# Hybrid decoder layer with hierarchical MoE: pair weights stored in four parts, first eight experts requested without a gather

## The reference

```
h  = rmsnorm(x, g_mix);  z = h @ w_in                    # 1024 -> 2048, four mixers of 256 columns
x  = x + concat(conv_a, pool, conv_c, gated_mlp) @ w_out
h  = rmsnorm(x, g_ffn)
g  = argmax of 4 group logits;  two best of the 8 experts of that group
w2 = softmax(two best logits) * softmax(group logits)[g]
x  = x + sum over the two experts of w2 * (silu(h @ w_gate) * (h @ w_up)) @ w_down
y  = rmsnorm(x, g_final)
```

## Time and profile before

| | us |
|---|---|
| median of 3 runs | 636.04 |
| lowest and highest of them | 634.98, 638.97 |
| profiled execution | 636.99 |
| span in its profile | 634.7 |
| busy TensorE products, share of the span | 570.7, 90% |
| busy VectorE, share | 462.3, 73% |
| busy ScalarE, share | 275.7, 43% |
| busy GpSimd, share | 143.8, 23% |
| moved by the transfers | 120.45 MB |

### The profile page before, as it was taken

One profiled execution on the slowest core, in us unless ns is written; L12 is line 12 of the kernel. 1 busy time (PEld: TensorE's weight loads), 2 busy tenths in 40 slices (PEclk: granted clock), 3 DMA queues, 4 the chain that ended last, 5 costly groups with the idle time before them and its releaser, 6 DMA issues.

```text
span 634.7 us, 10552 instructions
## 1 busy us (share of the span) xinstructions
PE 570.7 (90%) x3479; PEld 497.4 (78%) x3479; DVE 462.3 (73%) x726; ACT 275.7 (43%) x432; POOL 143.8 (23%) x178
## 2 busy tenths in 40 slices
PE   8899999999999998999999957999998989898800
PEld 6799999997998896888888746888877868677500
DVE  4938997999999668366665687888876756576525
ACT  6642112320413355322221265767765654565444
POOL 4300002000000000000000233656554545444200
PEclk9999999999999999999999969999999998899955
DMA  8760211120203204867443369999999999995359
GB/s 308 139 144 9 67 34 33 34 78 12 67 9 134 67 1 134 269 237 268 178 156 144 101 186 378 328 299 332 339 326 299 376 304 328 328 317 199 60 206 360
DMA packets 58023, 120.45 MB, mean 190 GB/s; under 512 B 12963, under 2 KB 31272, under 8 KB 57961
## 3 DMA queue, kind: packets, MB, share of 16 engines
q1 hardware_dynamic: 49077, 101.36, 46.9%
q0 software_dynamic: 6720, 17.85, 11.7%
q10 hardware_dynamic: 2164, 0.51, 0.4%
HBM read 95.19 MB, written 29.61 MB: 197 GB/s over the span
## 4 chain that ended last, share of the span: by engine, by line
PE 34%; SPq 19%; DVE 16%; DMA 7%; issue 3%; ACT 2%; POOL 0%; DVEq 0%; POOLq 0%; ACTq 0%
SPq L542 18%; PE ps L2123 13%; PE ps L1945 8%; DMA at_wfirst<-in_expert_w_up 3%; DVE at_mixP L1347 2%; PE ps L2272 2%; PE ps L2187 2%; PE ps L2248 1%; DVE at_x L1848 1%; PE ps L2250 1%; PE ps L2249 1%; DVE at_hT L1306 1%; DVE at_lnsq L1533 1%; DMA scratch_out<-at_outb,at_gcol 1%; PE ps L1873 1%
## 5 line engine op out<-in xcount | busy, mean ns | idle before, releaser
L1945 PE MATMUL ps<-at_hT,at_ring 128*128 128x384 f32 x936 | 164.8, 333 | 0.0
L1945 PEld LDWEIGHTS ps<-at_hT,at_ring 128*128 128x128 f32 x936 | 155.3, 188 | 5.2 <-issue 5.0
L2123 PE MATMUL ps<-at_hT,at_mring 128*128 128x512 f32 (+1 forms) x432 | 102.7, 393 | 2.0 <-DVE at_mring L1501 1.3
L2123 PEld LDWEIGHTS ps<-at_hT,at_mring 128*128 128x128 f32 (+1 forms) x432 | 77.3, 182 | 21.2 <-DVE at_mring L1501 1.7
L2248 PE MATMUL ps<-at_whi,at_hTm 128*128 128x256 f32 x280 | 83.1, 297 | 0.1
L2250 PE MATMUL ps<-at_whi,at_hTm_lo 128*128 128x256 f32 x280 | 80.8, 289 | 0.0
L1347 DVE SCALAR_TENSOR_TENSOR at_mixP<-at_uc,sb_par,at_mixP 128x1024 f32<-128x1024 f32 x60 | 77.4, 1289 | 2.1
L1188 POOL DMA_INDIRECT at_xg<-scratch_h,at_tab x32 | 54.8, 1713 | 72.1 <-DVE at_actv L1709 67.4
L1743 DVE TENSOR_TENSOR at_wlater_lo<-at_wlater,at_whi 128x1024 fp32r<-128x1024 f32 x40 | 48.8, 1221 | 25.3 <-ACT at_whi L958 25.1
L2248 PEld LDWEIGHTS ps<-at_whi,at_hTm 128*128 128x128 f32 x280 | 54.9, 196 | 0.6 <-DVE at_hTm_lo L1734 0.3
L2250 PEld LDWEIGHTS ps<-at_whi,at_hTm_lo 128*128 128x128 f32 x280 | 54.7, 195 | 0.0
(11 more groups left out here) (267 smaller groups left out, 859.6 us busy)
## 6 DMA issues: line engine op xcount, KB each, us to landing
at_wlater<-in_expert_w_gate SPq DMA_DIRECT2D x20, 512.0 KB, 10.6
at_wlater<-in_expert_w_up SPq DMA_DIRECT2D x20, 512.0 KB, 23.9
at_wlater<-in_expert_w_down SPq DMA_DIRECT2D x20, 512.0 KB, 24.2
at_raw<-in_w_in SPq DMA_DIRECT2D x16, 512.0 KB, 3.9
scratch_h<-at_wk SPq DMA_DIRECT2D x8, 1024.0 KB, 5.9
at_wfirst<-in_expert_w_gate SPq DMA_DIRECT2D x15, 512.0 KB, 9.4
at_wfirst<-in_expert_w_up SPq DMA_DIRECT2D x15, 512.0 KB, 21.3
at_wfirst<-in_expert_w_down SPq DMA_DIRECT2D x15, 512.0 KB, 21.3
```

The source lines that it names most:

```text
L1945: mm = pe.matmul(ps[:, bank + r, 0:t1 - t0], w[:, wpart, k * P:(k + 1) * P], hT[:, hpart, k, t0:t1], start=(m, wpart, hpart) == (0, 0, 0), ...
L2123: mm = pe.matmul(ps[0:n, b + r, :], mring[:, 1 - i % 2, mpart, k * P:k * P + n], wo[:, wpart, k, r * 512:(r + 1) * 512], start=(c, mpart, ...
```

## The change

The gates are stored in four parts instead of three: tiles 0 to 5, tile 6, tile 7, tile 8. ScalarE's queue stores part 0 as before and also the last part, behind its zeroing of the gather buffers; SP stores part 1 ahead of its wait for the last projection and part 2 where both of its parts were. A part of one tile is one store, so there are still five. GpSimd and ScalarE do their work for part 1 one stage earlier. On SP's queue the wait for the first gather is gone, and expert 5 is issued ahead of the store of x1 of tile 8.

```diff
-GATE_PARTS = [(0, 6), (6, LAST), (LAST, TILES)]
+GATE_PARTS = [(0, 6), (6, 7), (7, LAST), (LAST, TILES)]
...
             t0, t1 = GATE_PARTS[part]
             eng.wait_ge(s["gates_ready"], part + 1)
-            for k in range(1 if t0 == LAST else 2):
-                if t0 == LAST:
-                    dst = hs[2 * LAST * P:2 * NT, D:D + 1].rearrange("(p k) o -> p (k o)", k=2)
-                    src = gates[0:NS, LAST, :]
+            for k in range(1 if t1 - t0 == 1 else 2):
+                if t1 - t0 == 1:
+                    n = rows(t0)
+                    dst = hs[2 * t0 * P:2 * (t0 * P + n), D:D + 1].rearrange("(p k) o -> p (k o)", k=2)
+                    src = gates[0:n, t0, :]
...
             for i in range(TILES):
                 if i == LAST:
+                    store_gates(sp, 1)
                     sp.wait_ge(s["o_done"], TILES)
                     expert_block(0, FIRST, expert_at(FIRST), first=True)
...
-            for part in (1, 2):
-                store_gates(sp, part)
+            store_gates(sp, 2)
             expert_block(0, FIRST + 1, expert_at(FIRST + 1), first=True)
+            expert_block(0, FIRST + 2, expert_at(FIRST + 2), first=True)
             store_x1(LAST)
-            sp.wait_ge(gath[0], 16)
-            for j in range(FIRST + 2, LAP):
+            for j in range(FIRST + 3, LAP):
                 expert_block(0, j, expert_at(j), first=True)
...
                 if i == LAST:
                     store_gates(act, 0)
+                    gate_exp(1)
...
-            gate_exp(1)
+            gate_exp(2)
...
                 if n == 2:
-                    gate_exp(2)
+                    gate_exp(3)
...
                    s["xg_zero"])
+            store_gates(act, 3)
...
                 if i == LAST:
                     gate_values(0)
                     gate_terms(1)
+                    gate_values(1)
+                    gate_terms(2)
                 rms(1, i)
-            gate_values(1)
-            gate_terms(2)
             gate_values(2)
+            gate_terms(3)
+            gate_values(3)
```

## The result

The changed kernel takes 641.25 us (median of 11 runs, 637.53 to 643.83). The kernel before, run beside it, has a median of 637.27 us over 11 runs. The ratio is 1.0063, interval 1.0044 to 1.0081: the change costs 4.0 us (0.0063 of 637.27; 2.8 to 5.2). I had forecast 1.1 us less, with a range up to 638.7. The direction was wrong and the time lies outside the range. The outcome is nearest to rival C, to which I had given 0.18: the last tile's gates became the wait. The profiled execution took 642.72 us, with a span of 640.7.

What follows compares the result with a forecast made beforehand. The weight stream on SP's queue, with full DMA engines, was taken as the bound. Filling 2.8 us less 1.5 us new idle gave 1.3 us less, written as 634.9 us against 636.04, range 631.8 to 638.7.

Steps and rivals of the forecast that it cites:

- rival C: Last tile's gates, landing late beside weights, become the first gather's wait; d 6.8 us, loss 2.7 us, 638.7 us; chance 0.18.
- d: How much later the first expert ends, from later gathers and TensorE's clock: 2.8 us, bounds 0 to 5.5.
- Step 1: Tile 6's gates leave SP's late queue; their work and store fall into idle time, price zero.
- Step 2: Last tile's gates go from SP to ScalarE, landing about 378.4 us, 0.8 us before GpSimd's first gather starts.
- Step 3: Expert 4 asked for earlier on SP's queue fills idle DMA time before 388 us: gain 2.8 us, bounds 2.0 to 3.5.
- Rival D: Early weights only stand in their slots, as buffer release is the limit; time stays at 636.0 us; chance 0.12.
- Step 4: First gather meets weights, landing 2.0 us late; 2.3 us for two gathers plus 0.5 us for TensorE's clock dip.
- Rival B: Gather and gates share engines with weights packet by packet; d 0.8 to 1.5 us, about 633.5 us; chance 0.25.
- Step 5: Expert 8's weights wait for the late first expert's buffer, so the queue runs dry: 1.5 us of new idle.

Runs made afterwards that it cites:

- e1_wait_back: The changed kernel with SP's wait for the first gather put back ahead of experts 5 to 7; ratio 1.0050 to the kernel before, +3.2 us.
- e11_one_matrix_ahead: The changed kernel, but SP stores the last gates after only one of expert 4's three matrices, and waits for the first gather before experts 5 to 7; ratio 0.9989 to before.

## Why the prediction was wrong

**The bound was read rightly.** The engines of the transfers are full behind 406 us, expert 8's request ties the stream to the first gather, and a hole opens there. Break-even was put at d = 4.1 us, which is 30.2 us after H; the fit to the table has it at 29.2.

**Step 1** holds. SP issues tile 6's store at 364.68, in 0.52 us, and expert 3's loads are at 366.29, as before.

**Step 2 is the step that failed.** I took the last gates to land near 378.4 and to have 0.8 us in hand, because the store of before lands in 2.4 us. It landed at 381.92 and the gather started 3.7 us late. That row was of a store with no weights in front: in the order of before, SP's queue put the gates ahead of expert 4 by itself, and the change gave that up. The runs with 6.4, 6.6, 6.5 and 5.9 us behind expert 4 and 3.8 without it show it. The 0.8 us in hand were a misreading as well. What the gather of before had waited for is the first part of the table, done at 378.26, and it started 0.96 us after that:

```profile
378.07 0.19 DVE L1699 SCALAR_TENSOR_TENSOR at_tab<-at_empty,ps 128x36 int32<-128x36 f32 x1
```

In the changed kernel it started 1.02 us after the gates. So the gates had to land by about 378.2, before even the 378.4 that I took for them, and 381.92 is 3.7 us past that. Rival C described this wait and its place, and I gave it 0.18 on the strength of the later gathers, which are not tiny and are not the first to be waited for.

**Step 3** was right in itself: expert 4 at 372.43 (said 372.5 to 373.6), the last issue at 380.52 (before 381), 2.6 us filled (2.8), though 376 to 378 reached a share of 0.88 where I had said over 0.9. That filled time counts one for one was assumed and is not shown, since no kernel here both moved clearly more bytes than before by 408 us and was faster. Rival D, by which it counts for nothing, is not excluded.

**Step 4** was right: the gather took 8.21 us (said 7.8, bounds 5.0 to 9.6), 2.4 us late on that account, and a dip of the clock came. Rival B, which had the gather under 7 us, is out. The rest of the 7.3 us by which expert 8 is late is 7.3 - 3.7 - 2.4 = 1.2 us; I took 0.5 for the dip (bounds 0 to 1.7). The transposes alone took 1.6 us longer, so the dip can be all of it, but no run separates it.

**Step 5** had the right form. With d = 7.3, its sum gives 400.1 + 7.3 - 400.9 - 0.5 = 6.0 us of new idle and a loss of 3.2; the trace has 8.6, of which 2.6 off leaves 6.0. That is near the 5.7 us between the two profiled executions (642.72 and 636.99), which are not the medians; the ratio says 4.0. The gathers and scatters filled only 0 to 0.4 us of each window from 398 to 404.

**Rival C** named a price of 638.7 from d = 6.8, against 641.25 from d = 7.3. 1.2 us of the difference is before's own median, which went from 636.04 in three runs to 637.27 in eleven; the rest goes with the larger hole (8.6 us, where C had 5.5). That C's 4 us of delay is so near the 3.7 is partly luck. It had each element behind three weight packets; in the trace hardly any moved before 380 and then all within 2 us. Its 0.12 us for a tiny packet was misread too: in before, 144 packets took 6.8% of 376 to 377 us, 0.008 us each, and the other 16 of the earlier trace rows, 4 KB of weights each, took the rest. The upper end of the range was put at C's middle, not at its bound, and so left out the case that came. The 1% that I took for what can surely be told from no change was too wide: the intervals in the table are 0.13% to 0.29% to a side.

## What to carry to other kernels

Before a small transfer that everything waits for is moved to another queue, look at what its old queue kept behind it: on its own queue the order of issue protected it here, on another nothing did, and 1.5 MB issued up to 3 us earlier cost it 4 us. When a stall removed at the front of a saturated stream is to be a gain, ask which request is the first to depend on the work that is now competed with; a hole of 2.6 us was filled and one of 8.6 us opened 20 us later. A landing time is a price only for the company it was read in. And a share of busy time is not bytes: read the GB/s beside it.

## What the runs showed of the hardware that was not expected

A store of 128 single elements landed after 2.4 to 2.9 us where SP's queue had it ahead of expert 4 (seven kernels), 3.8 us with weight loads issued beside it on another queue, and 5.9 to 6.6 us with 1.5 MB issued in the 3 us or so before it, from ScalarE's or from GpSimd's queue alike. That the transfers ahead hold it is shown; by what means is open. In e1_wait_back the share had fallen to 0.41 in 380 to 382 and the store still landed only at 381.8. The length of TensorE's idle stretch alone does not tell whether the clock dips: before shows no dip after 2.94 us, e11_one_matrix_ahead shows one after 2.98 us, its clock at 0.50 from 386 to 390, though in both it stood at 1.00 in 382 to 384. That is one execution of each.
